# A hybrid trunk's router reordered, with unread products in its waits, two expert loops written out, and one split moved ahead in the dense layer

## The reference, cut to what matters

```python
def swiglu(h, wg, wu, wd):
    return (jax.nn.silu(h @ wg) * (h @ wu)) @ wd

def moe_swiglu(h, router, wg, wu, wd):
    logits = jnp.einsum('btd,de->bte', h, router).astype(F32)
    top_v, top_i = lax.top_k(logits, TOP_K)
    probs = jax.nn.softmax(top_v, axis=-1)
    combine = jnp.sum(jax.nn.one_hot(top_i, N_EXPERTS, dtype=F32) * probs[..., None], axis=-2)
    out = jnp.zeros_like(h)
    for e in range(N_EXPERTS):
        out = out + swiglu(h, wg[e], wu[e], wd[e]) * combine[..., e:e + 1].astype(h.dtype)
    return out
```

## Time and profile before

| | us |
|---|---|
| median of three runs | 2055.26 |
| the profiled execution's own time | 2050.26 |
| its span, first to last instruction | 2048.2 |
| TensorE busy in it | 2013.5 |
| VectorE busy | 1498.3 |
| ScalarE busy | 1181.0 |
| mean granted TensorE clock | 0.994 of full |

### The profile page before, as it was taken

The page is one execution under the profiler, slowest core; times in us unless marked ns, Lnnn a source line. Parts: engine busy times, 40 slices in busy tenths (PEclk is TensorE's granted clock), DMA queues, the critical chain, the costliest instruction groups (busy, mean ns, idle before and its releaser), DMA issues.

```text
span 2048.2 us, 32162 instructions
## 1 busy us (share of the span) xinstructions
PE 2013.5 (98%) x12798; PEld 1661.0 (81%) x12798; DVE 1498.3 (73%) x1491; ACT 1181.0 (58%) x1072; POOL 54.2 (3%) x56
## 2 busy tenths in 40 slices
PE   8999999999999999999999999999999999999998
PEld 8888989999999988889977777677776777777775
DVE  4767565656645656754768898888988888888887
ACT  4435444433334437444457777777767777677775
POOL 0200010000000020001000000000000000000000
PEclk9999999999999999999989999999999999999999
DMA  7423234445554533223449999899989999899995
GB/s 306 184 94 114 104 104 146 180 175 185 184 188 154 186 124 124 104 83 107 183 167 368 372 356 370 317 366 368 360 340 347 368 360 366 343 354 369 360 365 198
DMA packets 70796, 503.97 MB, mean 246 GB/s; under 512 B 8321, under 2 KB 8577, under 8 KB 9985
## 3 DMA queue, kind: packets, MB, share of 16 engines
q1 hardware_dynamic: 69792, 499.03, 64.9%
q10 hardware_dynamic: 864, 2.95, 0.4%
HBM read 500.90 MB, written 1.05 MB: 245 GB/s over the span
## 4 chain that ended last, share of the span: by engine, by line
PE 57%; DVE 2%; issue 1%; ACT 0%; DVEq 0%; ACTq 0%
PE g L506 36%; PE m L506 19%; PE m L1200 1%; DVE ring_low L2118 1%; DVE ring_low L2173 0%; PE m L777 0%; ACT we_high L1578 0%; PE m L550 0%; DVE arena L2026 0%; DVE h L2438 0%; DVE rstd L2436 0%; DVE rstd L1996 0%; DVE mg_low L2154 0%; PE m L1193 0%; DVE arena L2140 0%
## 5 line engine op out<-in xcount | busy, mean ns | idle before, releaser
L2173 DVE TENSOR_TENSOR ring_low<-ring,we_high 128x2048 fp32r<-128x2048 f32 x336 | 765.0, 2289 | 126.1 <-ACT we_high L1578 118.9
L1578 ACT ACTIVATE we_high<-ring 128x2048 fp32r<-128x2048 f32 x334 | 640.6, 1918 | 266.3 <-PE g L506 168.2
L506 PE MATMUL g<-we_high,hg_high 128*96 128x512 f32 x896 | 356.0, 397 | 2.9 <-DVE ring_low L2173 2.9
L506 PE MATMUL g<-ring_low,hg_high 128*96 128x512 f32 x896 | 353.0, 394 | 0.0
L506 PE MATMUL g<-we_high,hg_low 128*96 128x512 f32 x896 | 351.8, 393 | 0.0
L506 PE MATMUL g<-h_high,ring_low 128*128 128x256 f32 x1232 | 345.7, 283 | 0.0
L506 PEld LDWEIGHTS g<-h_high,ring_low 128*128 128x128 f32 x1232 | 231.9, 189 | 0.0
L506 PE MATMUL g<-h_high,w_high 128*128 128x256 f32 x720 | 201.1, 283 | 2.0 <-DVE ring_low L2191 1.9
L506 PE MATMUL g<-h_low,w_high 128*128 128x256 f32 x720 | 201.0, 283 | 0.0
L506 PEld LDWEIGHTS g<-we_high,hg_low 128*96 128x96 f32 x896 | 144.3, 161 | 63.4
L506 PEld LDWEIGHTS g<-we_high,hg_high 128*96 128x96 f32 x896 | 144.6, 161 | 62.7 <-issue 4.2
(11 more groups left out here) (320 smaller groups left out, 3169.5 us busy)
## 6 DMA issues: line engine op xcount, KB each, us to landing
ring<-stream SPq DMA_DIRECT2D x472, 1024.0 KB, 4.9
sw<-sw_in SPq DMA_DIRECT2D x1, 1088.0 KB, 11.2
sw<-sw_in ACTq DMA_DIRECT2D x1, 1088.0 KB, 8.1
x<-x_in SPq DMA_DIRECT2D x4, 256.0 KB, 4.3
out<-h ACTq DMA_DIRECT2D x4, 256.0 KB, 2.4
cc<-cc_in SPq DMA_DIRECT2D x1, 816.5 KB, 12.1
rep<-rep_in SPq DMA_DIRECT2D x1, 768.0 KB, 13.6
rep<-rep_in ACTq DMA_DIRECT2D x1, 768.0 KB, 8.4
```

The costliest lines, as they stand in the source:

```text
L506: return pe.matmul(o, a, b, start=start, stop=stop, skip_group_check=True)
L1578: A(we_high[n % 3][:, :], ring[:, slot, :], ACT.Copy).then_inc(high_ready, 1)
L2173: TT(ring_low[:, slot, :], ring[:, slot, :], we_high[n % 3][:, :], ALU.subtract).then_inc(low_ready, 1)
```

## The change

There are three places.

**Dense layer.** VectorE does `low(2)` ahead of the scaling of chunk 0, instead of after the three instructions on `first_gu`.

**Experts.** The two `Fori` loops of ScalarE and VectorE become Python loops, so the code of three turns stands in the program three times, with constants in the waits.

**Router.** Products that nobody reads (256 columns, high parts of the merge, into the unused half of bank `mbank[0]`) are put at three places on TensorE: 10 ahead of the last quarter of the sums, 10 after the transposes and ahead of the wait for the chosen experts, 8 after the counts. The last quarter's logits go ahead of its squares, and VectorE picks the best expert before it waits for the root. The flag's computation, one of the two first-half low parts and TensorE's wait for the flag move behind the matrices. The first gather is done in two halves, high and low parts of two banks together, each half with its own waits, into banks `mbank[0], gbank[0], gbank[2], gbank[3]`.

```diff
 def routed(i):                          # squares() and logits() as before
+    if i < 3:
+        squares()
+        logits()
     else:
+        logits()
+        squares()
...
 # gather, first
-                    for i in range(4):
-                        if i % 2 == 0:
-                            pe.wait_ge(S["htok_low_ready"], i + 2)
-                        for j in range(2):
-                            block(htok_high, i, j)
-                for i in range(4):
-                    for src in ((htok_low,) if first else (htok_high, htok_low)):
-                        for j in range(2):
-                            last = block(src, i, j)
-                    last.then_inc(S["hg_filled"], 1)
+                    m_done(pe, 1, "norm2")
+                some = 2 if first else 1
+                for i in range(0, 4, some):
+                    for src in (htok_high, htok_low):
+                        if first:
+                            pe.wait_ge(S["htok_high_ready"], i + 2)
+                            pe.wait_ge(S["htok_low_ready"], 1 if i == 0 and src is htok_high else i + 2)
+                        for k in range(i, i + some):
+                            for j in range(2):
+                                last = block(src, k, j)
+                            if src is htok_low:
+                                last.then_inc(S["hg_filled"], 1)
                 pe.wait_ge(S["comb_ready"], 1)
+                if first:
+                    pe.wait_ge(S["flag_ready"], 1)
...
+            def idle_products(n):
+                for _ in range(n):
+                    mm(mbank[0][:, T:2 * T], mg_high[:, 0, 0:P], mg_high[:, 1, :], False, False)
...
             def router():
+                idle_products(10)
                 routed(3)
                 tokens(1)
+                m_done(pe, 1, "norm2")
+                idle_products(10)
                 pe.wait_ge(S["chosen_ready"], 1)
...
-                pe.wait_ge(S["flag_ready"], 1)
+                idle_products(8)
                 pe.wait_ge(S["put_ready"], 2 * NCH)
-                pe.wait_ge(S["htok_high_ready"], 4)
                 gather(0, True)
...
 # ScalarE, VectorE
-                with act.Fori(0, E // 2 - 1) as pair:
+                for pair in range(E // 2 - 1):
...
-                with dve.Fori(0, E // 2 - 1) as pair:
+                for pair in range(E // 2 - 1):
...
 # VectorE, dense
-                    if n:
+                    if n > 1:
                         low(n + 1)
-                    else:
+                    elif n == 0:
+                        low(2)
                         dve.wait_ge(chunks_used, FFN0 + 1)
                         scale(first_gu.rearrange("p (j t) -> p j t", j=2), gbank[0], S["gu_scaled"])
...
 # VectorE, router
-                m_done(dve, 1, "norm2")
-                q.step(V.reciprocal(tok_scale, tok_rms), S["scale_ready"])
                 dve.wait_ge(m_filled[1], L * M_TOTAL[1] + 1)
...
                 pick(logits, v1, 1)
+                m_done(dve, 1, "norm2")
+                q.step(V.reciprocal(tok_scale, tok_rms), S["scale_ready"])
...
-                for c in range(NCH):
-                    htok_lows(0, c)
+                htok_lows(0, 0)
                 dve.wait_ge(S["counted"], 1)
                 q.step(TT(place_tok[:, :, 0:E], mbank[1][:, 16:32].rearrange("p (c e) -> p c e", c=NCH), r3(0), ALU.mult))
+                q.add(V.tensor_reduce(small[:, 80:81], mbank[1][:, 32:40], AX_X, ALU.max), v_seq)
                 put_tokens(0, True)
-                q.step(V.tensor_reduce(small[:, 80:81], mbank[1][:, 32:40], AX_X, ALU.max))
+                htok_lows(0, 1)
+                for c in range(NCH):
+                    htok_lows(1, c)
+                dve.wait_ge(v_seq, q.n[id(v_seq)])
                 q.step(V.tensor_scalar(small[:, 80:81], small[:, 80:81], CAP + 0.5, None, ALU.is_gt))
                 q.step(V.tensor_copy(flag[:, 0:1], small[:, 80:81]), S["flag_ready"])
-                for c in range(NCH):
-                    htok_lows(1, c)
```

More of the change, by code:

```diff
@@ L407, in gb, with gathered_in @@
             return gbank[G_PLAN[unit][0]]
+        def gathered_in(i, first):
+            return ((mbank[0], gbank[0], gbank[2], gbank[3])[i] if first else gbank[i])[:, 0:4 * CAP]
         def chunk0(l):
@@ L939, in routed, with squares, logits @@
             def routed(i):
-                pe.wait_ge(sq_ready, 4 * (2 * L - 1) + i + 1)
-                if i == 0:
-                    m_free(pe, 1, "norm2")
-                for c in range(NCH):
[L945 to L948, removed]
-                else:
-                    pe.wait_ge(m_drained[1], L * M_TOTAL[1])
-                pe.wait_ge(S["xg_ready"], 12 + i + 1)
-                for c in range(NCH):
[L953 to L957, removed]
+                def squares():
+                    pe.wait_ge(sq_ready, 4 * (2 * L - 1) + i + 1)
+                    if i == 0:
+                        m_free(pe, 1, "norm2")
+                    for c in range(NCH):
+                        for k in (2 * i, 2 * i + 1):
+                            last = mm(mbank[0][:, c * E:(c + 1) * E], sq[:, k, c * P:(c + 1) * P], ones[:, 0:E], c == 0 and k == 0, k == DT - 1)
+                    if i == 3:
+                        fill(1, "norm2", last)
+                def logits():
+                    if i == 0:
+                        pe.wait_ge(m_drained[1], L * M_TOTAL[1])
+                    pe.wait_ge(S["xg_ready"], 12 + i + 1)
+                    for c in range(NCH):
+                        for k in (2 * i, 2 * i + 1):
+                            last = mm(mbank[1][:, c * E:(c + 1) * E], xg[:, k, c * P:(c + 1) * P],
+                                      sw[:, SW["router"] + E * k:SW["router"] + E * (k + 1)], c == 0 and k == 0, k == DT - 1)
+                    if i == 3:
+                        last.then_inc(m_filled[1], 1)
+                if i < 3:
+                    squares()
+                    logits()
+                else:
+                    logits()
+                    squares()
             def tokens(i):
@@ L1087, in block @@
                     for c in range(NCH):
-                        last = mm(gbank[i][:, j * 2 * CAP:(j + 1) * 2 * CAP], src[:, c, k * P:(k + 1) * P], put_r[:, c, :],
+                        last = mm(gathered_in(i, first)[:, j * 2 * CAP:(j + 1) * 2 * CAP], src[:, c, k * P:(k + 1) * P], put_r[:, c, :],
                                   src is htok_high and j == 0 and c == 0, src is htok_low and c == 1)
@@ L1551, in dense, with gathered @@
                     high(n)
-            def gathered(pair_at):
+            def gathered(pair_at, first=False):
                 for i in range(4):
                     act.wait_ge(S["hg_filled"], pair_at(4, i + 1))
-                    A(hg_high[:, 2 * i:2 * i + 2, :], gbank[i][:, 0:4 * CAP].rearrange("p (j s) -> p j s", j=2), ACT.Copy)\
+                    A(hg_high[:, 2 * i:2 * i + 2, :], gathered_in(i, first).rearrange("p (j s) -> p j s", j=2), ACT.Copy)\
                         .then_inc(S["hg_high_ready"], 1)
@@ L1602, in experts @@
             def experts():
-                gathered(lambda n, c: c)
-                with act.Fori(0, E // 2 - 1) as pair:
+                gathered(lambda n, c: c, True)
+                for pair in range(E // 2 - 1):
                     for par in range(2):
@@ L2248, in put_tokens, with gathered @@
                         ins.then_inc(S["put_ready"], 1)
-            def gathered(pair_at):
+            def gathered(pair_at, first=False):
                 for i in range(4):
                     dve.wait_ge(S["hg_high_ready"], pair_at(4, i + 1))
-                    TT(hg_low[:, 2 * i:2 * i + 2, :], gbank[i][:, 0:4 * CAP].rearrange("p (j s) -> p j s", j=2),
+                    TT(hg_low[:, 2 * i:2 * i + 2, :], gathered_in(i, first).rearrange("p (j s) -> p j s", j=2),
                        hg_high[:, 2 * i:2 * i + 2, :], ALU.subtract).then_inc(S["hg_ready"], 1)
```

## The result

The first four executions of the changed kernel had a median of 2039.94 us (2039.63 to 2041.96), against 2053.11 us for the kernel before on the same chip: the ratio is 0.9934, with a 95% interval of 0.992 to 0.9949. In a later comparison eleven more executions had a median of 2043.60 us and a ratio of 0.9951 (0.9934 to 0.9969). All 15 together have a median of 2041.9 and a mean of 2042.9 us. The change makes the kernel faster by about 10 us, 0.5%.

The account below looks back on a forecast made before the run. TensorE's products bound the kernel, with gains in its holes and low-clock stretches. Loops 3.3, dense layer 3.3 and router 3.2 sum to 9.8 us, taken from the runs' median: 2045.5 us (chance 0.65), whole range 2039.8 to 2051.4.

Parts of the forecast that it names:

- Loops: Expert loops of VectorE and ScalarE written out: no turn ends in a jump back, 3.3 us won, bounds 0 and 3.3.
- Dense layer: Moving chunk 2's low part ahead removes TensorE's 1.87 us hole and the slow clock behind it: 3.3 us, bounds 1.6 and 3.3.
- The term of the clock: Dense layer, behind the hole before chunk 2: 13 fewer products at the fallen clock, 1.4 us that should go too.
- the fall follows the hole directly: Dense layer: reason for taking the full 3.3 us, the rows showing the clock falling right behind TensorE's hole.
- Router: New order and unread products start the first expert earlier: 3.2 us taken, midway between no half-clock stretch and one; bounds -0.4 and 3.9.
- Nothing else of this edit lies on the path: Expert loops: besides the jumps back, writing out changes no time, as the same instructions run and waits get constants.
- the starting value of the sum: Whole kernel: 9.8 us taken from the runs' median gives 2045.5 us; from the profiled execution's 2050.26 it gives 2040.5.
- The low end: Whole kernel: fastest time of the whole range, 10.5 us off the profiled execution, 2039.8 us.
- the low clock stays in the router in spite of the products: Router: clock falls for good, products cost instead of help, 6.2 us won in all, 2049.1 us; chance 0.2.
- the 4 us named as the sign of being wrong: Router: the forecast is wrong if the clock column shows the low level for more than 4 us.
- Holes from fetching the longer code: Experts: fetching two more turns' code while loads fill the DMA engines loses 14.7 us, kernel slower at 2060.2 us; chance 0.04.
- the stream: Experts: weight stream becomes the bound, or the hole has another cause; loops' gain fails, 6.5 us left, 2048.8 us; chance 0.08.

## Why the prediction was right or wrong

**Loops.** Forecast 3.3 us; 3.22 in the profiles (7.89 us earlier at expert 1, 11.11 at expert 5) and 3.2 with the edit alone. The cause, the hardware loop with its jump back, is shown.

**Dense layer.** Forecast 3.3. The times behind it are 3.6 to 3.7 us earlier (811.50 before, 807.86 after), and the edit alone gave 3.9. Wait, moved scaling and the table load under the wait went as worked out: the load at 405.19, the remainder of chunk 3 at 413.31 where 413.3 stood. The term of the clock was mis-sized: I counted missing products only from 412 to 416 and found 1.4 us, while the low stretch ran from 411.9 to 415.3, 3.4 us at half the rate, which is 1.7. The clock of 0.58 in the same row says so too: 0.42 of 4 us. And "the fall follows the hole directly" was a reading of one execution: it did in five profiles of six.

**Router.** Forecast 3.2, bounds -0.4 and 3.9. The order came out step by step, counted from the start of the last quarter's sums: chosen experts 3.8 us behind it, as forecast; counts from 1033.70 in 1.20 us; gather 6.3 us behind it where 6.7 was forecast, first expert 10.8 where 10.9 was. With the full clock the gain was 4.0 us by the chain, 0.1 above the bound. In expert 0 a further 0.2 us came (36 products in 8.43 us instead of 8.62). It goes with the loops and not with the router: the kernel with the whole router edit but the loops kept still has 8.62. At that place a ScalarE table load at the head of the first loop turn is gone, for which "Nothing else of this edit lies on the path" had left no cost. As a middle between clock levels 3.2 was fair. Eight profiles have the order and the products together. Four show no low clock in the router and lengths of 10.97 to 10.99 us, two show some 3.5 us of it and 12.50 and 12.57, and two show 6.8 and 6.9 us of it and 13.43. Against 14.97 that is a gain of 4.0, 2.5 and 1.5 us, and 3.0 in the mean (2.8 against the mean of the three profiles with the old router, 14.81).

**What failed was the start and the range.** The step that failed is the starting value of the sum. "Taken from the median the sum gives 2045.5 us" treated the runs' scatter as if it lay around a middle. The kernel before has two usual times, about 2051 and 2056, and the median of three (2055.26) was in the upper group while the profile was in the lower. Of the 5.6 us between the forecast and the measured 2039.94, 5.0 are this choice; from the profiled execution the same sum gave 2040.5. Taken from the mean of the 88 executions, 2053.6, it would have given 2043.8, against 2042.9 measured in the mean of 15. The first four executions of the changed kernel were also lucky: all 15 have a median of 2041.9.

The low end, "10.5 off the profiled execution, 2039.8", left nothing for terms above their bounds: the dense layer gave 3.6 where 3.3 was the bound, the router 4.0 where 3.9 was, expert 0 another 0.2. From profile to profile 11.1 us were won at the beginning of expert 5, and 0.7 lost behind the last product; the profiled execution's own time, 2039.63, lies under that end. The means differ by 10.7 us (2.1 either way); the forecast difference was 9.8. So the mechanisms and their sum held, and the clock's share of the time was not bounded as it should have been: the range knew of no low stretches outside the three places.

**The rivals.** That the low clock stays in the router in spite of the products happened in four of the eight profiles. In two of them it was more than the 4 us named as the sign of being wrong, but for 6.8 us and not for good, and even then 1.5 us were won instead of 0.4 lost. Holes from fetching the longer code did not come: in the first profile of the changed kernel TensorE waits for nothing from 1050 to 2020 us. For the same reason the stream is not the bound there: 84 chunks still take 246.4 us.

**Transposes and the clock.** By the Trainium skill, "TensorE: Matmul & The Clock Gate", Part 4: PE-mode transpose, transposes do not count as busy in the same way as other products. The profile with the low clock from 1032.9, just behind sums and transposes, fits that, but four of the eight profiles have the same transposes there and the full clock. No run separates transposes from small products, so it stays open which of them brings the clock down.

## What to carry to other kernels

Where one engine bounds a kernel and the others run in a hardware loop, look at the seam between two turns: a jump back cost VectorE 2.5 to 2.7 us and TensorE 1.5 to 1.7 us each time, and writing the loop out cost nothing measurable. A wait of TensorE can have a second price, the clock behind it: here 1.7 us behind a wait of 1.9, in five profiles of six. Full-width products that nobody reads, put into a wait that is there anyway, can shorten the time at the low clock and cost next to nothing (0.06 us in mixer D), but only judge them over many executions and with the mean clock beside each time.

## What the runs showed that I had not expected

The places at which the clock falls differ between executions of one kernel, and between edits that do not touch them. The profiles showed low stretches at 103, 195, 342, 735, 826, 970 and 1019 us, each 3.4 us long, or 6.8 to 6.9, 10.2 to 10.3 and once 13.6. The longest was in mixer D of the kernel with the products alone, from 734.5 to 748.1. Times and mean clocks of the executions fit that such stretches make the two usual times of the kernel before, but it has only one profile, so which ones do is not shown. What a stretch costs depends on its place. Compared product by product, one of 3.4 us cost 1.5 to 1.7 us at 103, 342, 412 and 970, but 0.1 us at 825 and nothing measurable at 195, where TensorE waits for VectorE soon after. The one of 13.6 us cost 6.6. An edit of 1 or 2 us can be hidden by them in one profile: the loops alone had their 3.2 us, and a span 2.5 us longer than that of the kernel before.
